# A blocked RWKV-7 recurrence: two small steps of the inverse, each half a slot later

## The reference, cut to what matters

```python
def wkv7_scan(r, decay, k, v, kk_neg, kk_b, reverse):
    def step(state, inp):
        r_t, w_t, k_t, v_t, an_t, b_t = inp
        sa = jnp.einsum('bhij,bhj->bhi', state, an_t)
        state = (state * w_t[:, :, None, :] + sa[..., None] * b_t[:, :, None, :]
                 + v_t[..., None] * k_t[:, :, None, :])
        return state, jnp.einsum('bhij,bhj->bhi', state, r_t)
...
    for direction, reverse in ((0, False), (1, True)):
...
        y = y + wkv7_scan(heads(r), heads(decay), heads(k_dir), heads(v), -kk, kk * heads(a), reverse)
```

## Time and profile before

| | |
|---|---|
| time, median of 3 runs | 4709.09 us (4706.46 to 4734.16) |
| time of the profiled execution | 4716.15 us |
| its span on the core | 4714.4 us |
| TensorE, matmuls busy in the span | 4143.5 us (88%) |
| VectorE busy | 2915.9 us (62%) |
| ScalarE busy | 2228.8 us (47%) |
| GpSimd busy | 1175.0 us (25%) |

### The profile page before, as it was taken

How to read it: one execution, slowest core, us unless ns; L and a number is a source line. 1 busy time by engine, 2 the same in 40 slices (tenths; PEclk the granted TensorE clock), 3 DMA queues, 4 the chain that set the end, 5 groups by cost and what they waited for, 6 DMA issues and landing times. The chain is left out here.

```text
span 4714.4 us, 123717 instructions
## 1 busy us (share of the span) xinstructions
PE 4143.5 (88%) x50861; PEld 3797.6 (81%) x50862; DVE 2915.9 (62%) x5152; ACT 2228.8 (47%) x4176; POOL 1175.0 (25%) x954
## 2 busy tenths in 40 slices
PE   6979999975999968888888869944999999999998
PEld 5869999965888856667676747734999999999998
DVE  5879999965888854444444447756444444444443
ACT  4568888854666633333333322201444444444443
POOL 4544444421344420110102223301112112112111
PEclk9989999998999979999999979966999999999999
DMA  8920000014444332222222246603556556556554
GB/s 167 187 61 26 22 23 26 23 32 136 144 153 143 127 133 67 66 66 64 67 64 67 60 124 203 196 25 95 168 175 180 170 172 184 168 171 184 170 172 108
DMA packets 555357, 540.74 MB, mean 115 GB/s; under 512 B 80320, under 2 KB 502464, under 8 KB 554944
## 3 DMA queue, kind: packets, MB, share of 16 engines
q1 hardware_dynamic: 489920, 435.44, 29.6%
q10 hardware_dynamic: 50240, 52.44, 4.9%
q0 software_dynamic: 14784, 46.57, 4.8%
HBM read 377.92 MB, written 156.43 MB: 113 GB/s over the span
## 5 line engine op out<-in xcount | busy, mean ns | idle before, releaser
L2298 DVE TENSOR_TENSOR g_wlo<-g_raw,g_whi 128x2048 fp32r<-128x2048 f32 x192 | 439.1, 2287 | 115.3 <-ACT g_whi L2260 115.3
L2260 ACT ACTIVATE g_whi<-g_raw 128x2048 fp32r<-128x2048 f32 x192 | 366.4, 1908 | 145.0 <-DMA g_raw<-expert_w_gate 145.0
L2369 PE MATMUL g_pD<-g_whi,g_hh 128*128 128x256 f32 x1536 | 417.3, 285 | 2.5 <-ACT g_o L2287 2.4
L2369 PE MATMUL g_pD<-g_wlo,g_hh 128*128 128x256 f32 x1536 | 408.1, 279 | 0.0
L1119 PE MATMUL c_pP<-c_xh,c_whi 128*128 128x258 f32 x1120 | 328.6, 293 | 34.7 <-DMA c_gup<-g_lora_up 29.3
L587 DVE TENSOR_TENSOR sapl<-sapT,saph 128x512 fp32r<-128x512 f32 x512 | 329.9, 686 | 2.7 <-ACT saph L546 2.7
L577 DVE TENSOR_REDUCE sanm<-sapS 128x1 f32<-128x1024 f32 x256 | 313.5, 1225 | 25.8 <-PE sapS L628 15.8
L2231 POOL DMA_INDIRECT g_x<-hn_rows,index x48 | 69.4, 1446 | 1035.2 <-PE g_pU L2353 1024.9
L546 ACT ACTIVATE saph<-sapT 128x512 fp32r<-128x512 f32 x512 | 278.8, 596 | 94.1 <-PE sapT L640 94.0
L1344 POOL TENSOR_TENSOR d_kr<-d_kr,d_fixed 128x512 f32<-128x512 f32 x80 | 101.8, 1273 | 880.0 <-ACT d_kr L1370 880.0
L1119 PE MATMUL c_pP<-c_xh,c_wlo 128*128 128x258 f32 x1120 | 319.9, 286 | 0.0
(11 more groups left out here) (369 smaller groups left out, 12445.8 us busy)
## 6 DMA issues: line engine op xcount, KB each, us to landing
g_raw<-expert_w_gate SPq DMA_DIRECT2D x64, 1024.0 KB, 5.0
g_raw<-expert_w_up SPq DMA_DIRECT2D x64, 1024.0 KB, 8.3
g_raw<-expert_w_down SPq DMA_DIRECT2D x64, 1024.0 KB, 5.0
ops<-c_ops SPq DMA_DIRECT2D x40, 1024.0 KB, 4.2
d_bd<-ops SPq DMA_DIRECT2D x160, 256.0 KB, 3.1
c_xh<-xT_hi SPq DMA_DIRECT2D x10, 1032.0 KB, 5.8
c_xl<-xT_lo SPq DMA_DIRECT2D x10, 1032.0 KB, 9.2
x_in<-x SPq DMA_DIRECT2D x20, 512.0 KB, 8.2
```

The costliest lines, as they stand in the source:

```text
L2260: act.activation(w_hi[:, Q % NBUF, :, :], raw[:, Q % NRAW, :, :], ACT.Copy).then_inc(s["g_hi"], 1)
L2298: dve.tensor_tensor(w_lo[:, Q % NBUF, :, :], raw[:, Q % NRAW, :, :], w_hi[:, Q % NBUF, :, :].bitcast(F32), ALU.subtract).then_inc(s["g_lo" ...
L2369: mm = pe.matmul(pD[k][:, 0:WB], x[:, d, k * P:(k + 1) * P], w[:, b, d, :], start=(d == 0 and i == 0), stop=(d == DC - 1 and i == len(part ...
```

## The change

Each of the two steps moves by half a slot. On TensorE, `squared` stood in slot 5, part 1, of the chunk before, and stands in slot 0, part 0; `fours` stood there, and now stands in slot 0, part 1, ahead of `through`. On VectorE `smallest` moves from slot 5, part 1, to slot 0, part 0. On ScalarE the copy `fours` moves from slot 0, part 0, to slot 0, part 1, ahead of `known`. The two calls ahead of the loop fall away. No instruction is added or removed, and the waits inside the steps stay as they are.

```diff
@@ ScalarE
             def run(m, par, i, l, part, g):
                 if part == 0:
-                    if l == 0 and is_chunk(m):
-                        fours(m, par, g)
                     if l > 0 and is_chunk(m):
                         stationary(m, par, l - 1, g)
                     if l == STEPS - 1 and is_chunk(m + 1):
                         keys(m + 1, 1 - par, g)
                 else:
+                    if l == 0 and is_chunk(m):
+                        fours(m, par, g)
                     if l == 0 and is_chunk(m - 1):
                         known(m - 1, g)
@@ VectorE
                 if part == 0:
+                    if l == 0 and is_chunk(m):
+                        smallest(m, g)
                     if 0 < l <= NL and is_chunk(m):
                         between(m, l - 1, g)
...
                     if 0 < l <= NL and is_chunk(m):
                         grown(m, par, l - 1, g)
-                    if l == STEPS - 1 and is_chunk(m + 1):
-                        smallest(m + 1, g)
 
             reads(0, 0, 0)
-            smallest(0, 0)
             order(dve, staggered(run))
@@ TensorE
                 if part == 0:
                     if l == 0 and is_chunk(m):
-                        fours(m, g)
+                        squared(m, g)
...
                 else:
+                    if l == 0 and is_chunk(m):
+                        fours(m, g)
                     if l == 0 and is_chunk(m - 1):
                         through(m - 1, 1 - par, g)
...
                     if 0 < l <= NL and is_chunk(m):
                         grown(m, par, l - 1, g)
-                    if l == STEPS - 1 and is_chunk(m + 1):
-                        squared(m + 1, g)
 
             x12(0, 0, 0)
-            squared(0, 0)
```

## The result

| | before | changed |
|---|---|---|
| time, median of 20 runs each, taken together | 4712.95 us (4689.61 to 4743.38) | 4745.87 us (4723.0 to 4775.29) |
| ratio to before, 95% interval | | 1.0058 (1.0038 to 1.0078) |
| span of the profiled execution | 4714.4 us | 4748.2 us |
| steady recurrence, from the third to the last d_few | 974.6 us | 1007.4 us |
| of it halves 0 (39), halves 1 (38) | 533.2, 441.4 us | 555.4, 452.0 us |

The change makes the kernel slower. The ratio of 1.0058 is 27 us; the two medians lie 33 us (0.70%) apart, and both sizes are inside the interval, which reaches from 18 to 37 us. Later the changed kernel was timed a second time, on another occasion: 1.0042 (1.0017 to 1.0066), with a recurrence of 1004.7 us. Of the 33.8 us between the two profiled spans 32.8 us lie in the recurrence. The length of a half is the time from one start of d_few on VectorE to the next.

A forecast was written before the change was run, and what follows sets the result against it. TensorE, in-order and waiting for other engines, was taken as the engine to fill. Terms of 18, 6 and 1.5 us gave +25.5 us on the 4709.09 us median: 4734.6 us, range 4692 to 4768 us.

The forecast's parts named there:

- halves 0: Halves of a period (one chunk of each direction) in which direction 0 starts a chunk; forecast 0.46 us longer each.
- halves 1: Halves of a period in which direction 1 starts a chunk; forecast +6 us and +1.5 us in all.
- The freed wait: Rival: in half 0 `out` starts when TensorE reaches it, saving the 1.13 us wait and square; 4686 us, chance 0.08.
- The product in half 0: `fours` ahead of `through` is exposed: 0.55 us less 0.09 us saved at `out`, 0.46 us each, +18 us.
- The square in half 1 costs nothing: Removing it from behind `out` leaves about 1.8 us idle and saves nothing; it takes the place of `fours` at no cost.
- the product is hidden: In half 1, `fours` ahead of `through` fits into TensorE's idle time before `between` of level 3, in 28 halves.
- the cover: Idle time in half 1 that hides the 0.55 us of `fours`; counted present in 28 halves, missing in 11.
- the 0.58 us wait: TensorE's idle time in half 1 before `between` of level 3, released by d_z; forecast to shrink to about 0.2 or less.
- Regular halves 1 as long as before: Sign to look for in the changed kernel's profile: regular halves 1 do not lengthen.
- The rival with the falling clock: Longer idle stretches make TensorE fall to half clock more often; up to 30 us more, 4765 us, chance 0.15.
- the uncovered product: In half 1, 11 halves without cover pay 0.55 us, +6 us; thinner ones among 28 miss some 0.05 each, +1.5 us.
- The rule on the clock: Frequent short idle times between matmul groups swing the clock between two levels; by it the clock rival decides, 4765 us.

The follow-up runs named there:

- d_pm early: Changed kernel with d_fewT and d_one moved out of `reads` on VectorE to the slot's second part, so d_pm comes right behind d_br; 1.0047 of before.
- product only: Kernel before with only the 4x4 blocks' product and its ScalarE copy half a slot later, square and its sum unmoved; 0.9971 of before.
- the filler runs: Changed kernel plus idle TensorE products in half 1's idle stretch: 24 small ones, 1.0081 of before; three wide ones, 1.0035.

## Why the prediction was right, and where it was not

The forecast was +25.5 us; measured are +27 us by the ratio and +33 by the medians (by the ratio +20 us the second time). The sign, the size and the two waits that changed hands came out. The parts of the sum did not come out as well as the sum: one was too large and one left out, so that its closeness is in part luck.

- **The freed wait is not real.** Right. The 1.13 us became a wait of 1.13 us for d_pm, 39 times; forecast was 1.04. The difference is the release, taken as 0.06 us from the end of d_fewT to the square; from the end of d_pm to `out` it is 0.14. "d_pm early" shows the cause by experiment.
- **The product in half 0, +0.46 us each, +18 us.** Right in mechanism, too large in size by the cleanest pair. With the same waits in both halves it is 0.25 us, 10 us in all; the medians of the regular halves differ by 0.27 to 0.36. The term that was mis-sized is the product's time on TensorE, taken as 0.55 between 0.41 and 0.60. In its new place `between` of level 2 gives way 0.25 us behind its start (0.35 before), and the product 0.38 us behind its own: `through` is 0.28 us later, less than the lower bound. Both bounds had come from rows with other neighbours. The sums of halves 0 rose by 14 to 22 us; what is above 10 is not resolved from the scatter of stalls (26 us of them in halves 0 before, 31 in both traces of the changed kernel) and clock.
- **The square in half 1 costs nothing, the product is hidden.** The product is hidden in the halves that have the cover: those without a fall, a stall or a slow d_st last 10.50 us in both kernels, and the 0.58 us wait is gone. Where a stall of 0.85 to 0.90 us falls into `through` the product does cost, 0.41 and 0.45 us in two pairs of halves 1 that are alike otherwise, where 0.55 was forecast: 11.34 us before (from 1775.01) against 11.75 changed (1775.63), and 11.45 before (2102.09) against 11.90 in the second trace (2139.68). The count of 28 halves with a wait of 0.4 to 0.6 us took in six of 1.1 to 1.6 us, those of the slow d_st; they have more cover, not less. That the square takes the place of the product at no cost is right against the kernel before, but the place itself is worth 0.35 us, as "product only" shows; the change as a whole could have been a gain of 0.3%, and moving the square there spent it.
- **"Regular halves 1 as long as before."** Right for those in which the clock holds, wrong for most. The rival with the falling clock, given 0.15, happened in over half of them: 22 and 20 early falls of 38 against 3. This is the term that the sum put at nothing. The longest single idle time went from 0.62 to 1.90 us at that point. One fall costs 1.3 us in its half. Halves 1 rose by 11 to 16 us in sum, where the forecast had 7.5 for other reasons (the uncovered product), and the early falls cost some 1.3 us each in their halves, so this part came near by chance. Half clock in all rose from 122 to 143 and 154 us, less than the 60 us more on which the rival's 4765 us rested, since the later falls in halves 1, 9 before, went down to 1 and 4.
- **The rule on the clock in the Trainium skill** (page "TensorE: Matmul & The Clock Gate", section "A second HAM failure mode: psum-queue depth-cycling") was weighed as a rival. The traces agree that a short idle time is enough: the fall behind 2197 follows 1.90 us of idle, and 22 such falls become 1 when that time is filled. That it decides the size of the whole change is not borne out by the filler runs.
- **The median against which it was stated.** The 4734.6 us were set on 4709.09, the median of 3 runs; with 20 runs it is 4712.95. The forecast by its own terms would have been 4738.5 against 4745.87.

What stays open: how much the clock costs the kernel within the estimated bound of 16 and 11 us, what lengthened the halves 0 by more than the product, and what the stalls without releaser are. They fell into halves 0 and 1 of both kernels, and rose with the fillers; no run varied them by themselves.

## What to carry to other kernels

When a wait of the bounding engine is to be removed, read in the code what the next instruction waits for as well, and find that operation in the queue of its own engine: here d_pm, 0.50 us behind the one that was waited for, kept the place of the whole gain. Look also at what an operation is in front of: a step that is not itself late can be in the way of one that feeds a chain, and one half of a two-part move can be worth more alone (0.9971) than both together (1.0058). Two short idle times with work in between are not the same as one long one of the same total, since the clock can fall behind the long one. And a move on one engine can put two operations of different engines beside each other that slow each other: look at the duration of each moved operation, not only at the waits.

## What was not expected of the hardware

- The clock fell for about 3.4 us behind an idle stretch of 1.90 us that followed dense work, in 20 to 22 of 38 places, and in 3 of 38 where the same stretch was split into 0.60 and 0.62 us with a square between (in 9 in "product only", which has the same split, so one trace gives a rough count). With 1.45 us of idle it was 8, with 1.03 us it was 6.
- In these traces an operation of VectorE with both inputs in SBUF that stood beside an operation of GpSimd was held until that one was over: d_st 1.35 us in place of 0.43, d_one 1.19 in place of 0.38, each ending 0.28 or 0.29 us behind the GpSimd operation. Those with one input in PSUM were not: at 2067.78 in the changed kernel d_yo takes its 0.42 and d_z its 0.28 us beside the d_kr step of GpSimd.
- The start of a group of eight 64x64 products behind another depends on the neighbours: 0.60 us from the square to `out`, 0.41 to `state`, 0.38 to `through`.
- Filling an idle stretch of TensorE with work brought more stalls without a releaser elsewhere, 69 to 74 us in place of 51 to 55, with 48 and also with only 6 more instructions per place. The cause is not known.
